# Attention block on one core: the sum-of-squares matmul of the seventh weight tile moved ahead of a_mix 1, in all four heads

## The reference, cut to what matters

```python
hn = rmsnorm(h, g_norm[l])
proj = hn @ w_in[l]                                   # 1024 x 1024 by 1024 x 4352
aq, ak, av, ag, bq, bk, bv, bg, mq, mg = jnp.split(proj, IN_SPLITS, axis=-1)
a_out = swa_sink_attention(aq, ak, av, a_sinks[l], a_slopes)      # band of two chunks of 64
lam = jnp.exp(jnp.sum(lq1 * lk1)) - jnp.exp(jnp.sum(lq2 * lk2)) + lam_init
b_heads = diff_attention(bq, bk, bv, lam, b_slopes)               # softmax 1 - lam * softmax 2
b_out = rmsnorm(b_heads, b_subln_g[l]) * (1.0 - lam_init)         # over the 128 values of a head
m_out = memory_attention(mq, rmsnorm(mem, g_mem[l]), w_mem_kv[l]) # 256 memory tokens
gated = jnp.concatenate([a_out * silu(ag), b_out * silu(bg), m_out * silu(mg)], axis=-1)
h = h + gated @ w_out[l]
return rmsnorm(h, g_final)
```

## Time and profile before

| what | value |
|---|---|
| median of 3 runs | 704.76 us |
| the profiled execution | 704.69 us, its span 702.9 us |
| TensorE busy | 692.9 us, 99% of the span |
| VectorE busy | 420.1 us, 60% |
| ScalarE busy | 311.8 us, 44% |
| GpSimd busy | 231.4 us, 33% |
| share of TensorE in the chain that ended last | 91% |
| granted TensorE clock over the span | 0.999 of full speed |

### The profile page before, as it was taken

The page is one execution under the profiler, slowest core; times in us unless marked ns, Lnnn a source line. Parts: engine busy times, 40 slices in busy tenths (PEclk is TensorE's granted clock), DMA queues, the critical chain, the costliest instruction groups (busy, mean ns, idle before and its releaser), DMA issues.

```text
span 702.9 us, 11709 instructions
## 1 busy us (share of the span) xinstructions
PE 692.9 (99%) x3989; PEld 582.3 (83%) x3989; DVE 420.1 (60%) x922; ACT 311.8 (44%) x729; POOL 231.4 (33%) x204
## 2 busy tenths in 40 slices
PE   8999999999999999999999999999999999999996
PEld 8988888888888888888888888888888887888885
DVE  6786246766754666675466667635667786433332
ACT  7753444455543444564344556334454654122200
POOL 5723132144333214333331434233243543222310
PEclk9999999999999999999999999999999999999999
DMA  9921212020052101005211110421140285514210
GB/s 298 309 62 30 61 32 60 1 60 2 1 151 61 40 21 43 19 1 151 61 30 31 31 31 1 146 65 30 31 124 5 61 273 153 158 60 129 81 59 37
DMA packets 79158, 52.73 MB, mean 75 GB/s; under 512 B 36081, under 2 KB 71937, under 8 KB 79105
## 3 DMA queue, kind: packets, MB, share of 16 engines
q1 hardware_dynamic: 79104, 52.06, 25.8%
HBM read 43.14 MB, written 8.91 MB: 74 GB/s over the span
## 4 chain that ended last, share of the span: by engine, by line
PE 91%; DVE 6%; ACT 2%; issue 1%; DVEq 0%; POOL 0%; ACTq 0%; POOLq 0%
PE acc L1490 18%; PE acc L1491 17%; PE acc L1492 17%; PE score L1490 4%; PE score L1492 3%; PE score L1491 3%; PE trans L1492 3%; PE trans L1490 3%; PE trans L1491 3%; PE score L1684 2%; PE score L1686 2%; PE trans L1704 2%; PE mixo L1491 2%; DVE logits L1393 2%; PE mixo L1492 2%; PE mixo L1490 2%
## 5 line engine op out<-in xcount | busy, mean ns | idle before, releaser
L1490 PE MATMUL acc<-x_hi,w_hi 128*128 128x512 f32 x544 | 217.3, 400 | 0.2 <-DVE gates L1258 0.2
L1491 PE MATMUL acc<-x_lo,w_hi 128*128 128x512 f32 x544 | 212.8, 391 | 0.0
L1492 PE MATMUL acc<-x_hi,w_lo 128*128 128x512 f32 x544 | 212.5, 391 | 0.0
L926 POOL TENSOR_TENSOR w_lo<-w_raw,w_hi 128x512 fp32r<-128x512 f32 x66 | 85.0, 1308 | 175.4 <-ACT w_hi L604 156.6
L1492 PEld LDWEIGHTS acc<-x_hi,w_lo 128*128 128x128 f32 x544 | 102.1, 188 | 22.2
L1490 PEld LDWEIGHTS acc<-x_hi,w_hi 128*128 128x128 f32 x544 | 102.3, 188 | 20.6 <-issue 1.9
L1491 PEld LDWEIGHTS acc<-x_lo,w_hi 128*128 128x128 f32 x544 | 102.4, 188 | 17.9
L773 ACT ACTIVATE logits<-logits,stats_b 128x128 f32<-128x128 f32 (+7 forms) x64 | 49.2, 770 | 50.4 <-DVE stats_b L1287 50.4
L1279 DVE CUSTOM_DVE_ANT_0 logits<-score,b_bias 128x384 f32<-128x384 f32 (+5 forms) x96 | 50.0, 554 | 23.1 <-PE score L1686 22.6
L782 ACT ACTIVATE p_hi<-trans 128x512 fp32r<-128x512 f32 (+1 forms) x56 | 30.8, 565 | 63.4 <-PE trans L1704 42.1
L1306 DVE TENSOR_TENSOR p_lo<-trans,p_hi 128x512 fp32r<-128x512 f32 (+1 forms) x56 | 35.8, 651 | 33.6 <-ACT p_hi L782 33.2
(11 more groups left out here) (249 smaller groups left out, 1359.3 us busy)
## 6 DMA issues: line engine op xcount, KB each, us to landing
w_raw<-in_w_in SPq DMA_DIRECT2D x68, 256.0 KB, 3.4
mixed<-gates SPq DMA_DIRECT2D x9, 512.0 KB, 4.2
mix_raw<-mixed SPq DMA_DIRECT2D x8, 576.0 KB, 5.8
wo_raw<-in_w_out SPq DMA_DIRECT2D x8, 512.0 KB, 6.7
x_res<-in_x SPq DMA_DIRECT2D x8, 512.0 KB, 3.4
out_y<-y_row SPq DMA_DIRECT2D x16, 256.0 KB, 2.1
logits<-in_x SPq DMA_DIRECT2D x4, 512.0 KB, 7.9
wo_raw<-in_w_out SPq DMA_DIRECT2D x6, 256.0 KB, 5.9
```

Source lines behind the costliest of these rows:

```text
L926: last = pool.tensor_tensor(w_lo[:, slot, cols], w_raw[:, slot, cols], w_hi[:, slot, cols].bitcast(F32), ALU.subtract)
L1490: pe.matmul(out, a_hi, b_hi, start=start, stop=False, skip_group_check=True)
L1491: pe.matmul(out, a_hi, b_lo, start=False, stop=False, skip_group_check=True)
L1492: return pe.matmul(out, a_lo, b_hi, start=False, stop=stop, skip_group_check=True)
```

## The change

In the list behind quarter 1 of the second half of weight tile 6, `b_squares 0` is taken from behind `a_mix 1` and put in front of it. `a_mix 1` and `a_scores 3` then follow each other on TensorE. Nothing else differs.

```diff
@@ -78,7 +78,7 @@
     (6, 0, 2): [("b_mix", 3, 0), ("m_norm", 0)],
     (6, 0, 3): [("b_spread", 3, 3), ("b_mix", 3, 1), ("b_fold", 0)],
     (6, 1, 0): [("b_mix", 3, 2), ("m_spread", 0), ("b_mix", 3, 3), ("m_scores", 1), ("b_low", 0)],
-    (6, 1, 1): [("a_mix", 1), ("b_squares", 0), ("m_norm", 1), ("a_scores", 3), ("m_scores", 2), ("a_spread", 2)],
+    (6, 1, 1): [("b_squares", 0), ("a_mix", 1), ("m_norm", 1), ("a_scores", 3), ("m_scores", 2), ("a_spread", 2)],
     (6, 1, 2): [("a_norm", 3), ("m_spread", 1), ("m_norm", 2), ("m_mix", 0)],
     (7, 0, 0): [("m_scores", 3), ("b_fold", 1)],
     (7, 0, 1): [("a_mix", 2), ("m_norm", 3), ("m_spread", 2)],
```

## The result

The changed kernel took 707.55 us (median of 7 runs, 707.16 to 708.18), the kernel before 705.06 us on the same chip (median of 7, 704.46 to 705.83). The ratio is 1.0035, with a 95% interval of 1.0025 to 1.0045: 2.5 us slower, between 1.8 and 3.2. The forecast was 706.9 us, 2.2 us more than before.

What follows compares the result with a forecast made beforehand. TensorE, 99% busy, was taken to bound the kernel. Waiting for L1379, less saved crossings, loses about 0.55 us in each of four heads, 2.2 us on the profiled 704.69 us: 706.9 us, range 706.1 to 707.8.

Steps and rivals of the forecast that it cites:

- The bound: Inside the heads TensorE, busy 692.9 of 702.9 us, sets the pace; any wait of it is lost in full, once per head.
- The added wait: The moved sum of squares would be ready at 166.96 but waits for L1379, ending 167.53; TensorE idles, once per head.
- The sum: First quarter's last matmul to m_scores 2: hold, sum of squares, a_mix 1, a_scores 3; loss 0.54 to 0.56 us per head.
- the sum of squares starts at 167.53 + 0.05: First head: held matmul starts 0.05 us after L1379 ends at 167.53, a release time read at L1258.
- the cover's surplus: Before the change, a_mix 1's 0.63 us covered L1379; the sum of squares started 0.14 us after L1379 ended.
- The second term, refill and entry: Held sum of squares lasts 0.23 plus 0.11 refill plus 0.09 going into the small group, 0.43 us.
- The forecast of standing still 0.62 us to save 0.08 us: Plain summary of the per-head trade on TensorE: 0.62 us idle at the moved matmul against 0.08 us saved.
- The crossings: Around the sum of squares, one way out of and one into small matmuls fall away: 0.19 us gain per head.
- rival 3: Boundary between 128x64 and 64x64 groups costs a drain, up to 0.19 us more per head, 707.7 us; chance 0.06.
- Rival 1: L1379's result comes in time in most heads, so only the 0.19 us per head gain counts: 704.0 us; chance 0.04.
- Rival 2: Held matmuls at L1200 and L1258 come without a wait, taking back some 1.5 us: 705.5 us; chance 0.06.
- The DVE swap: L1387 ahead of L1318 on DVE costs nothing; m_probs ready about 170.4, over 1 us before its transposes.

Runs made afterwards that it cites:

- pe_swap_only: Changed kernel with DVE put back to the old order, so only TensorE's order differs from the kernel before: 708.07 us, ratio 1.0039.
- after_stt_low: Changed kernel with L1379 written as scalar_tensor_tensor (times 1.0, minus) instead of tensor_tensor: ratio 1.0040 to the kernel before.
- dve_swap_only: Kernel before with only DVE in the order of the change (L1387 ahead of L1318), TensorE as before: 705.16 us against 705.28, ratio 0.9997.

## Why the prediction was right, and where it was not

**The bound.** That TensorE sets the pace inside the heads, so that a hold counts in full, held: the four places add up to 2.39 us, the kernels with TensorE's new order and the same hold lie 2.5 us (the change) and 2.8 us (pe_swap_only, after_stt_low) over before, and the profiles show about 0.1 us given back between the heads.

**The added wait.** Right. It appears four times, with 2.3 us in all, and goes with `b_low 0` brought forward.

**The sum.** Its direction and nearly its size were right, 0.54 to 0.56 us per head predicted and 0.59 to 0.61 measured, but two of its terms were off. The step "the sum of squares starts at 167.53 + 0.05" failed: the distance from the end of L1379 to the held matmul is 169.08 - 168.94 = 0.14 us in the first head, and the same in the others. The price of 0.05 us came from a place with one wait, and the sum of squares has two. The prediction had the right number before it, 0.14 us in both heads of the kernel before, and read it as the cover's surplus. It was the distance of a matmul that is being released: doubling L1379 in the kernel before cost 0.60 of its 0.61 us. The profile names no wait for L1792 there, because a_mix 1, shown with 0.69 us, fills the time up to it. The second term, refill and entry, was put at 0.20 us (0.43 for the matmul) and is 0.17 (0.40 us from L1792 to L1784). The two errors point opposite ways, 0.09 us too little and 0.03 us too much, so the sum came out nearer than its first term.

With that, the sum becomes simpler than the one predicted. In both kernels L1792 starts 0.14 us after L1379, at the same moment, and takes nearly the same time (0.42 before, 0.40 after). Behind it stands a_mix 1 with 0.62 us that used to be done by then. 0.62 - 0.02 = 0.60 us is the loss. The median lies 0.6 us over the 706.95 us that the prediction gave for it; 0.3 us of that is the kernel before, whose median was 705.06 us in this comparison and 704.76 us in the runs that the forecast started from. The forecast of standing still 0.62 us to save 0.08 us becomes 0.72 us (0.96 less a matmul's 0.24) to save 0.12.

**The crossings.** Right: 0.19 us predicted, 0.20 with the wait taken away (0.15 in the fourth head), 0.19 at the pair that was separated, and the change has them too, only hidden by the refill.

**The boundary between the two forms (rival 3).** It costs nothing in this order either: a_mix 1 takes 0.62 us and a_scores 3 0.59 us standing together in the changed kernel. The rule of the Trainium skill, TensorEngine Tiling (Array Packing), section Key Properties, that a change of tiling mode drains TensorE, agrees with the trace between full and small matmuls, at about 0.09 us in and 0.10 us out; between 128x64 and 64x64, in either order, no time for it shows here.

**Rival 1**, that the wait doesn't bind, was out. The experiment that made its condition true gave no gain all the same, because m_scores 2 was held in turn. **Rival 2**, the loss taken back downstream: the waits for L1200 and L1258 are 0.7 and 0.2 us as before. The 0.3 us between the heads are mostly the spot at 326.23 us in the profile of the kernel before, and not a gain of the change.

**The DVE swap** cost nothing, as costed: dve_swap_only is at 0.9997, and in the changed kernel m_probs is ready at 170.79 + 1.04 = 171.83 while its transposes start at 173.34.

## What to carry to other kernels

When a step is moved ahead of another, look at what the other one covered: here 0.6 us of small matmuls hid the last of a chain on DVE, and saving 0.2 us of mode crossings uncovered it. A consumer that starts the same short time after its producer in every repetition (0.14 us, four times) may have nothing to spare: here it was released by it, though no wait was named, and making the producer later showed it. To bring two steps together, move the third one behind both rather than in front, and check that its reader can follow.

## What was not expected of the hardware

- The distance from the recorded end of a DVE instruction to the start of the matmul that waits for it is not one number: 0.05 us behind L1258 (float32 output) and L1200 (float32r output), 0.14 to 0.15 us behind L1379 and L1105. The kind of instruction makes no difference, and both distances occur with a float32r output on 128 rows. It goes with whether the wait stands on the weight load or in an instruction of its own in front of it.
- A DVE instruction can start before the recorded end of the one before: L1380 and L1382 of the doubled subtraction, 0.69 and 0.68 us long, start 0.61 us apart.
- Two executions of the same prologue leave TensorE up to 1.4 us apart, because the entry of full clock begins anywhere between 4.47 and 7.62 us. It is over half of what this change costs, and enough to mislead whoever compares two single profiles by their spans.
